# Masking the state-space decay products: from a TensorE product with a matrix of -1e30 to masked CB and a clamped exponent on VectorE

## The reference, cut to what matters

```python
seg = a_cs[..., :, None] - a_cs[..., None, :]
decay = jnp.exp(jnp.where(causal, seg, -jnp.inf))
cb = jnp.einsum('bclgn,bcsgn->bcgls', cm, bm)
y_diag = jnp.einsum('bcgls,bcgjls,bcsgjp->bclgjp', cb, decay, xdt)
```

## Time and profile before

| | |
|---|---|
| median of 3 runs | 1735.07 us (1733.42 to 1736.85) |
| the profiled execution's own time | 1738.51 us |
| its span, from first to last instruction | 1736.9 us |
| TensorE busy over the span | 1632.0 us, 94% |
| VectorE, ScalarE, GpSimd busy | 663.8, 414.0, 284.0 us |
| the state-space stage | about 81 to 590 us of the span |
| a group's head part (groups 0 to 2; group 3) | about 45.7 us; 42.7 us |

### The profile page before, as it was taken

One profiled execution on the slowest core, in us unless ns is written; L12 is line 12 of the kernel. 1 busy time (PEld: TensorE's weight loads), 2 busy tenths in 40 slices (PEclk: granted clock), 3 DMA queues, 4 the chain that ended last, 5 costly groups with the idle time before them and its releaser, 6 DMA issues.

```text
span 1736.9 us, 23551 instructions
## 1 busy us (share of the span) xinstructions
PE 1632.0 (94%) x9244; PEld 879.6 (51%) x9245; DVE 663.8 (38%) x1089; ACT 414.0 (24%) x770; POOL 284.0 (16%) x311
## 2 busy tenths in 40 slices
PE   6999999999999999999999999999999979999893
PEld 3464564564565444445455454445566565555441
DVE  2444544554544646000166673013224132222224
ACT  4334433423433310000133234101010121111112
POOL 0005406406406400000000000000000032212212
PEclk9999999999999999999999999999989989999997
DMA  9800200200210474211111011216233279997994
GB/s 345 313 22 27 69 21 33 73 31 19 97 45 4 163 263 156 97 50 49 48 49 49 1 49 63 83 48 214 94 145 139 104 279 363 358 375 285 394 351 157
DMA packets 105907, 239.96 MB, mean 138 GB/s; under 512 B 5393, under 2 KB 14870, under 8 KB 105842
## 3 DMA queue, kind: packets, MB, share of 16 engines
q1 hardware_dynamic: 86800, 180.60, 28.9%
q0 software_dynamic: 14288, 48.96, 7.9%
q10 hardware_dynamic: 4754, 9.49, 1.5%
HBM read 217.01 MB, written 22.02 MB: 138 GB/s over the span
## 4 chain that ended last, share of the span: by engine, by line
PE 85%; DVE 7%; DMA 2%; ACT 2%; issue 2%; POOL 1%; ACTq 0%; DVEq 0%; POOLq 0%
PE psum L450 17%; PE psum L1142 9%; PE psum L464 9%; PE psum L810 6%; PE psum L657 6%; PE psum L1166 4%; PE psum L454 4%; PE psum L925 3%; PE psum L561 2%; PE psum L705 2%; PE psum L739 2%; PE psum L959 2%; PE psum L857 1%; DMA arena<-exp_w_d 1%; PE psum L714 1%
## 5 line engine op out<-in xcount | busy, mean ns | idle before, releaser
L450 PE MATMUL psum<-arena 128*128 128x512 f32 x688 | 300.9, 593 | 3.6 <-DVEq L417 2.8
L450 PEld LDWEIGHTS psum<-arena 128*128 128x128 f32 x688 | 128.1, 189 | 160.1 <-issue 154.2
L1142 PE MATMUL psum<-arena 128*32 128x256 f32 x2816 | 166.4, 388 | 5.9 <-issue 5.3
L464 PE MATMUL psum<-arena 128*128 128x512 f32 x352 | 152.7, 593 | 0.0
L1142 PEld LDWEIGHTS psum<-arena 128*32 128x32 f32 x2816 | 92.3, 111 | 64.8 <-issue 12.4
L657 PE MATMUL psum<-arena 128*128 128x512 f32 x256 | 118.8, 596 | 0.0
L810 PE MATMUL psum<-arena 128*128 128x512 f32 x256 | 111.5, 593 | 0.0
L464 PEld LDWEIGHTS psum<-arena 128*128 128x128 f32 x352 | 66.4, 190 | 80.5 <-issue 80.4
L1802 DVE SCALAR_TENSOR_TENSOR arena<-arena 128x772 f32<-128x772 f32 (+1 forms) x96 | 93.9, 978 | 3.4
L2384 POOL TENSOR_TENSOR arena<-arena 128x512 f32<-128x512 f32 x64 | 87.7, 1390 | 45.4 <-ACT arena L1450 45.4
L2346 POOL TENSOR_TENSOR arena<-arena 128x512 f32<-128x512 f32 x40 | 41.3, 1041 | 277.5 <-ACT arena L1390 272.5
(11 more groups left out here) (377 smaller groups left out, 2114.3 us busy)
## 6 DMA issues: line engine op xcount, KB each, us to landing
arena<-exp_w_d SPq DMA_DIRECT2D x48, 2048.0 KB, 16.0
arena<-w_in_d SPq DMA_DIRECT2D x22, 2048.0 KB, 8.0
arena<-ada_w_d POOLq DMA_DIRECT2D x8, 2048.0 KB, 9.9
slots<-arena POOLq DMA_DIRECT2D x1, 9216.0 KB, 26.9
arena<-ada_w_d SPq DMA_DIRECT2D x4, 2048.0 KB, 20.4
arena<-ssd_proj_d SPq DMA_DIRECT2D x4, 2048.0 KB, 11.1
slots<-arena POOLq DMA_DIRECT2D x92, 64.0 KB, 5.0
arena<-slots POOLq DMA_DIRECT2D x22, 256.0 KB, 6.0
```

The costliest lines, as they stand in the source:

```text
L450: ins = mmul(ps[:, 0:T], slot[:, k, m * P:(m + 1) * P], src[:, k, C:NT], start=(k == 0), stop=(k == KD - 1))
L464: ins = mmul(ps[:, 0:n], src[:, k, t * P:(t + 1) * P], slot[:, k, 0:n], start=(k == 0), stop=(k == KD - 1))
L1142: ins = mmul(psU[q * R:(q + 1) * R, 0:2 * HF], XT[:, k % 2, k // 2, :], w13[p][:, :, k, q * HF:(q + 1) * HF], start=(k == 0), stop=(k == K ...
```

## The change

The mask leaves the exponent. Each row product is one matmul, with nothing added. The exponent can then be large and positive where it does not count, so VectorE takes the minimum with zero in place (a second instruction a pair, which must wait for the subtraction's result), and raises a semaphore of its own for ScalarE. What must not count is taken out through `cb`, of which there are now two, one for each direction, both multiplied by the 0/1 mask when VectorE reads them from PSUM. GpSimd's product reads `cb[d]`. The two `shut` tiles and their setup are gone; `rrow` shares memory with `vtmp`, to make room for the second `cb`.

```diff
-        cb = alloc(TL, P)
+        cb = [alloc(TL, P) for _ in range(2)]
...
-        rrow = alloc(T)
+        rrow = vtmp
...
                     mmul(ps[:, :], selb[0:3 * SH, hh:hh + 1].to_broadcast([3 * SH, P]),
-                         rowsT[0:3 * SH, d, :], start=True, stop=False)
-                    ins = mmul(ps[:, :].rearrange("p (c l) -> p c l", c=TL), identb,
-                               shut[d].unsqueeze(1).to_broadcast([P, TL, P]), start=False, stop=True)
-                    ins.then_inc(is_full(key)[0], 1)
+                         rowsT[0:3 * SH, d, :], start=True, stop=True).then_inc(is_full(key)[0], 1)
...
-                        act.wait_ge(*is_free(("R", g, d, h)))
+                        act.wait_ge(S_("exponent_ready"), n + 1)
...
-            for d in range(2):
-                v.tensor_scalar(shut[d], mask[d], -1.0, 1e30, ALU.add, ALU.mult)
...
-                v.tensor_copy(cb, bank(key)[:, :].rearrange("p (c l) -> p c l", c=TL)).then_inc(is_free(key)[0], 1)
+                for d in range(2):
+                    ins = v.tensor_tensor(cb[d], bank(key)[:, :].rearrange("p (c l) -> p c l", c=TL),
+                                          mask[d].unsqueeze(1).to_broadcast([P, TL, P]), ALU.mult)
+                ins.then_inc(is_free(key)[0], 1)
...
+                    dve.wait_ge(*is_free(key))
+                    v.tensor_scalar(mm[n % NM], mm[n % NM], 0.0, None, ALU.min).then_inc(S_("exponent_ready"), 1)
...
-                        g_.tensor_tensor(mm[n % NM], mm[n % NM], cb, ALU.mult).then_inc(S_("M_ready"), 1)
+                        g_.tensor_tensor(mm[n % NM], mm[n % NM], cb[d], ALU.mult).then_inc(S_("M_ready"), 1)
```

More of the change, by code:

```diff
@@ L190, in build @@
         dtT = yT[0:2 * SH, 4:6, :].rearrange("p a b -> p (a b)")[:, 0:NT]
-        rrow = alloc(T)
+        rrow = vtmp
         ssum = alloc(T)
         d_col = small[:, 0:SI // P]
-        shut = [tmpd[0].rearrange("p t h -> p (t h)")[:, 0:P].bitcast(BF16)[:, d * P:(d + 1) * P] for d in range(2)]
         assert RAW % 2 == 0
```

## The result

The changed kernel takes 1746.3 us (median of 6 runs, 1744.01 to 1747.44) against 1733.97 us before (6 runs, 1733.35 to 1736.85). The ratio is 1.0058, 95% interval 1.0043 to 1.0072: slower by 7.5 to 12.5 us (the two medians lie 12.3 apart). The profiled execution took 1746.80 us, where that of the kernel before took 1738.51.

A forecast was written before the change was run, and what follows sets the result against it. TensorE, busy 1632 of 1736.9 us, was taken as the bound. Groups 0 to 2 at +0.8 each and group 3 at +1.4 gave +3.8 on 1735.07: 1738.9 us, own range 1736.5 to 1741.5, 8-in-10 range 1731 to 1746.

The forecast's parts named there:

- rival 3: Unrelated holds: each of six minima a group waits 0.54 us, not 0.12; +2.5 a group, 1749 us, chance 0.12.
- What is taken away: 64 mask products on TensorE, 0.22 us each in a running stream; ceiling 14.1 us, 3.5 a group.
- (a): Start of a group's head part: TensorE is spared nothing, 2.51 us becomes 2.62, +0.1.
- (b): Head-part steps b = 0 to 2: VectorE's path +0.05 and GpSimd's holds 0.25 a step; +0.9 for three.
- (c): Step b = 3, without L714: TensorE keeps most of its 0.43 us if GpSimd is in time; -0.3.
- (d): First pair of direction 1: TensorE ahead by only 0.18 of the 0.43 us spared; -0.2.
- (e): Row products of direction 1's later pairs: a pair spares 0.22 us; those of the last pair come at -0.2.
- (f): Last pair's chain to L739: loses a mask product, gains a minimum with its wait and a GpSimd hold; +0.5.
- (g): Group 3, less for TensorE to do, already waiting for GpSimd: +0.6 at first pair, then the chain; +1.4.
- (h): The rest, such as VectorE reading CB twice, 0.69 us more a group under idle time: costs nothing.
- 1: Rival: minima not held by GpSimd; sum -1.0, 1734.1 us, no change; chance 0.26.
- 2: Rival: TensorE's spared time comes through, -2.0 a group, -8 us, 1727 us; chance 0.14.

The follow-up runs named there:

- e3: Changed kernel with subtraction and minimum fused into one instruction, four of 128 columns a head, reading PSUM; 1741.96 us, ratio 1.0035 against the kernel before.
- e2: Kernel before, mask products kept, with the changed kernel's minima added; 1750.16 us, ratio 1.0090 against the kernel before.
- e6: Kernel before with only the two masked copies of CB, mask products kept; 1733.63 us against 1733.65, ratio 1.0010.
- e1: Changed kernel without minima, exponents divided by 64, so other expert choices; 1734.23 us (1744.09 for the kernel before with the same division), head parts 9.1 us shorter than before.
- e5: Changed kernel with fused PSUM instructions except in a group's first pair, evacuation between a step's two heads; 1727.81 us, ratio 0.9967 against the kernel before.
- e4: Changed kernel with VectorE's order in a step changed alone: both subtractions, evacuation of state_off, both minima; 1738.75 us, ratio 1.0018 against the kernel before.

## Why the prediction was right in kind and too small

The direction was right. The measured time, 1746.3, lies 0.3 us above the range of 1731 to 1746; by the ratio it is +7.5 to +12.5 us for a forecast of +3.8, and by the head parts, which the sum spoke of, +8.3. The forecast's own range, 1736.5 to 1741.5, was missed. That the wide range reached so far was owed to rival 3, whose share it held, and not to the sum.

- **What is taken away.** Right: row products start 0.22 us apart, and 64 matmuls are gone.
- **The minimum's length**, 0.43 us estimated from 364 and 563 ns, is 0.43 (median 430 ns) where GpSimd leaves it alone.
- **(a)** +0.1 forecast; 2.51 us before, 294.12 - 291.61 = 2.51 after: 0. TensorE is spared nothing there, as said.
- **(b)** is the step that failed, in one term. The path was right: VectorE's L1879 is what the state product waits for, and TensorE's 0.43 a step is gone before any contention (without holds, in e3, a step is 5.45 us for 5.48 before). The minima are held, as forecast. The size of the hold was not: "held, 0.12 each, so 0.25 a step". In the step shown the first minimum is held for 0.98 - 0.43 = 0.55 and the second for 0.55 - 0.43 = 0.12, 0.67 in all.

  The argument that the two engines fall into step after one hold was right for the second minimum, which follows a hold, and wrong for the first, which is held for 0.35, 0.55 and 0.66 us in the three steps. Between the steps VectorE waits for TensorE while GpSimd works on without a gap, so the two do not start together. What the first minimum waits for is what its step is short of GpSimd's round: 6.29 us with the mask products (e2, held 0.44) and without them (held 0.66). The prediction counted that round at 5.5 us, with products of 1.25, though its own rows had one of 1.72; it was 5.92 before and is 6.29 with the minima in it. It saw that GpSimd "is always at work", but not that holding a minimum in TensorE's way makes GpSimd's round the step.

  The three steps cost +2.3 us a group (`y_part(0, 2)` 22.20 us after the start of the part and not 19.87), of which 1.9 are holds, and not +0.9. Rival 3 had the size of it, half an instruction, but for all six minima and as a matter of chance; the trace shows a fixed pattern, much the same in all four groups. By rival 3's own test, a mean hold over 0.25 us, the trace speaks for it: the six minima are held 0.32 on average.
- **(c)** -0.3 forecast, -0.43 measured: 25.53 - 22.20 = 3.33 us from y to y, where it was 3.76.
- **(d)** -0.2, measured -0.18: from the `y_part` before, 5.37 us after, 5.55 before. **(e)** -0.2, measured -0.3 over the next two pairs.
- **(f)** +0.5, measured +0.49: `y_part(1, 3)` follows the one before it after 4.38 and not 3.89 us, with 1.45 us of waiting in place of 0.96. The chain, from the changed kernel's list in order of time, beside the earlier trace rows:

```profile
332.75 0.70 DVE arena L1907
...
333.47 0.44 DVE arena L1910
...
333.94 0.64 ACT arena L1446
...
334.64 3.14 POOL arena L2383 x2
```

- **(g)** +1.4 forecast, +2.63 measured; 1.9 of it is there at the first pair of direction 1, that is (a) to (c) again, and 0.75 the chain's own, close to the 0.8 forecast.
- **(h)** Right: e6 measured nothing for it.
- **The signs.** Those named came as named, but for one: TensorE's idle time before `state_kv` was to be some 0.4 us and is 0.58, 0.91 and 1.02 in the steps of group 1. The last wait is 1.45 for 1.4 and over, and group 3 waits 4.6 us for GpSimd, for over 4.

So groups 0 to 2 came to +1.9 and not +0.8, group 3 to +2.6 and not +1.4. The difference of 4.5 us is, roughly, the holds of the first minimum in the twelve steps, some 5 us longer in all than forecast, less what (a), (c) and (e) came out lower. Of the rivals, 1 is out (the minima are held), and 2 is out for this kernel, though e1 and e5 show that its premise, TensorE's time in the masks, is worth 9 and 7 us when neither VectorE's path nor a hold stands in the way. What stays open: 1.8 us between the head parts (+8.3) and the middle of the measured interval (+10.1); it lies within the interval, and no run was made for it. And no run made GpSimd's round itself shorter or longer; that it is the step rests on e2 and the changed kernel having the same 6.29 us, and on e3, where nothing is held.

The Trainium skill (SBUF — State Buffer, Who interferes with whom) states the hold for one-source instructions in a two-port mode, and that an instruction with at most one SBUF input, outside those modes, does not contend with GpSimd. The runs now agree with both halves: 0.43 to 1.44 us for the minimum, and 335 to 353 ns for all 256 fused ones, which read PSUM.

## What to carry to other kernels

Work moved off a busy engine lands in another's queue: before it is called idle, follow who stands behind the new instruction there and who waits for that one. Here an engine busy for 55% of the head part, held up by one busy for 71%, decided the time of one busy for 96%. The price of such a VectorE instruction from SBUF to SBUF beside GpSimd was its length plus what GpSimd's instruction had left: 0.78 to 1.09 us for the first minimum of a step in group 1, in place of 0.43. Where GpSimd never rests, add up its round too (here 6.29 us): an instruction that it holds, in the way of the busy engine, makes that round the length of the step. Reading PSUM avoided the hold (e3), and putting the instruction that others wait for first took it out of the way of the state product (e4). And a kernel with routing in it can only be timed against one with the same values.

## What the runs showed of the hardware

TensorE's clock fell in the middle of a dense stage. In group 2 of e3 it fell after 1.26 and 0.46 us of idling with only two row products before and one between, in group 3 after 1.30 and 0.42, at a cost of 1.2 and 1.7 us; in groups 0 and 1 the same waits (1.27 and 1.26, then 0.46) left it at 1.00. The changed kernel had waits of 0.82 and 0.49 at that place, and stayed at 1.00 through its whole stage. In e4 it fell in group 3 (0.51 over 3.5 us) after a wait of 1.91 us for GpSimd; the changed kernel had the same 1.91 there and stayed at 1.00. So the same waits can come with a fall or without one.

A VectorE instruction that GpSimd holds ties VectorE's pace to GpSimd's: in the changed kernel and in e2, whose TensorE orders differ by the mask products, the steps are the same 6.29 us.
